# The low halves of six weight granules move from VectorE to GpSimd in the recurrence of a two-layer trunk

## The chip, the cores and the metric

The kernel runs on one core of one Trainium2 chip. The metric is the device time of one execution in microseconds (us).

## The reference

Two layers on 256 tokens of width 1024, all in float32, batch 1. Layer 0 is a gated mixer, a dense SwiGLU and a gated embedding. Layer 1 is an HGRN2 recurrence, a top-2-of-8 expert SwiGLU and a gated embedding. The change lies in the recurrence:

```python
def hgrn2(h, w_in, lb, o_norm_g, w_out):
    q, f, i, g = jnp.split(h @ w_in, 4, axis=-1)
    forget = lb + (1.0 - lb) * jax.nn.sigmoid(f)
    log_f = jnp.log(forget)
    k = 1.0 - forget
    q = jax.nn.silu(q)
...
    def step(state, inp):
        qc, kc, ic, lfc = inp
        b = jnp.cumsum(lfc, axis=2)
        o_inter = jnp.einsum('bhtk,bhkv->bhtv', qc * jnp.exp(b), state)
        attn = jnp.einsum('bhtk,bhsk,bhtsk->bhts', qc, kc, decay)
        o = o_inter + jnp.einsum('bhts,bhsv->bhtv', attn, ic)
...
    o = rms_norm(o, o_norm_g)
    return (o * jax.nn.silu(g)) @ w_out
```

## The kernel before, in words

**Weights.** Every weight matrix is streamed in granules of 128 partitions by 2048 float32 columns, in two halves of 1024 columns. For granule `g`, SyncE's queue loads each half into a slot of `raw`; ScalarE writes its rounded copy `w_hi` (`hi(g)`, L984); VectorE writes the rest, `w_lo = raw - w_hi` (`lo(g)`, L1362). TensorE multiplies three times: high by high, high by low and low by high (L460, L461, L462). The two halves of a product so keep float32's precision. `w_hi` and `w_lo` have six slots. `raw` has three before the experts begin (granule 72), so that the load of granule `g` waits for `lo_done` of granule `g - 3`. `lo_done` is one semaphore that counts halves in the order of the granules. TensorE waits for it too, and `hi(g)` waits for `used` of granule `g - 6`.

**The recurrence.** Granules 52 to 67 are its input projection (`G_INC` is 52): 52 to 55 give f, 56 to 59 q, 60 to 63 i, 64 to 67 g. Granules 68 to 71 are its output projection (`G_OUTC` is 68). The decayed products of q and k are built in levels 0 to 7, which halve the block on which they work. TensorE multiplies in a level (`level(n)`: L707 for level 0, L726 for 1 to 5, L719 for 6, L712 for 7), VectorE scales half of q and of k for the next level (L1685, L1686), signals `qk_ready`, forms the next block products (L1691), and merges the level's result into `attn` under a mask (`meet`, L1666). Between two levels TensorE has the projection of half a granule (`proj_part`, 12 matmuls). So level n + 1 waits for VectorE's two multiplications, and these wait for level n and for all that stands before them in VectorE's order. In that order stand `lo(64)` ahead of level 1's loop, and `lo(65)` to `lo(69)` at the end of the turns 2 to 6.

TensorE's order from level 3 on: level 3, half of granule 63, level 4, half of 64, level 5, half of 64, level 6, half of 65, level 7, half of 65, the products with the values (L770), the product across the two tiles (L782), and granules 66 and 67.

**GpSimd** sets constants up at the start and then issues DMAs. Its third gain is loaded once `gain_free` is 2, its fourth once `gain_free` is 3, after the recurrence's output norm.

Of the kernel before, what the change touches and what calls it, by code (L numbers as in the profile page):

```python
# [22 lines left out]
ALU = mybir.AluOpType  # L23
ACT = mybir.ActivationFunctionType
AXX = mybir.AxisListType.X
F32 = mybir.dt.float32
# [6 lines left out]
RING = 6  # L33
RAW = 3
GW = 2048
HW = GW // 2
# [7 lines left out]
def trunk(nc, x_d, pT_d, columns_d, norm_g, w_in_ab, a_ln_g, a_ln_b, wsT_d, w_out_ab, ffn_w_gu,  # L44
# [23 lines left out]
    G_INC = G_PLE0 + 5  # L68
    G_OUTC = G_INC + 16
    G_MOE = G_OUTC + 4  # L70
    assert G_MOE % RING == 0 and ITEM % RING == 0 and G_MOE % RAW == 0

    with ExitStack() as ctx:
# [7 lines left out]
        w_hi = sb("w_hi", [P, RING, GW], F32R)  # L81
        w_lo = sb("w_lo", [P, RING, GW], F32R)
# [149 lines left out]
        def raw_part(g, s):  # L232
            k = raw_slot(g)
            return raw[:, k, s * HW:(s + 1) * HW] if k < RAW else more_raw[k - RAW][:, s * HW:(s + 1) * HW]
# [19 lines left out]
        def o_bank(t):  # L254
            return 4 + 2 * t
# [125 lines left out]
        @block.gpsimd  # L381
        def _(pool):
            count = [0]

            def step(ins):

                count[0] += 1
                ins.then_inc(pool_step, 1)
                pool.wait_ge(pool_step, count[0])

            step(pool.memset(ident[:, :], 0.0))
            step(pool.affine_select(out=ident[:, :], in_=ident[:, :], compare_op=ALU.not_equal, fill=1.0, base=0,
                                    pattern=[[-1, P]], channel_multiplier=1))
            step(pool.memset(ones[:, :], 1.0))
            step(pool.affine_select(out=before[:, :], in_=ones[:, :], compare_op=ALU.is_gt, fill=0.0, base=0,
                                    pattern=[[1, P]], channel_multiplier=-1))
            pool.memset(zeros[:, :], 0.0).then_inc(consts, 1)
            pool.iota(iota_c[:, :].bitcast(I32), pattern=[[1, P]], base=0, channel_multiplier=0).then_inc(seg_in, 1)
            pool.iota(rt[:, 0:P].bitcast(I32), pattern=[[0, P]], base=0, channel_multiplier=1).then_inc(seg_in, 1)
            pool.wait_ge(lo_done, 2)  # L400
            pool.dma_start(wr[:, :, :], w_router).then_inc(router_full, 16)
            pool.dma_start(br[:, :], b_router[0:1, :].broadcast_to([P, E])).then_inc(router_full, 16)
            pool.dma_start(wsT, wsT_d).then_inc(ws_full, 16)
            pool.dma_start(lng, a_ln_g[0:1, :].broadcast_to([P, AW])).then_inc(ln_full, 16)
            pool.dma_start(lnb, a_ln_b[0:1, :].broadcast_to([P, AW])).then_inc(ln_full, 16)
            gains = [norm_g[0, 1:2], norm_g[0, 3:4], norm_g[1, 1:2], norm_g[1, 3:4]]
            for n, v in enumerate(gains):
                if n:
                    pool.wait_ge(gain_free, n)
                pool.dma_start(gain[:, :], v.broadcast_to([P, D])).then_inc(gain_full, 16)  # L410
                if n == 2:
                    pool.dma_start(ybuf[0:ROWS, :].rearrange("(p a) (b c) -> p (a b) c", p=P, c=N // 2),
                                   zeros[:, :].bitcast(F32).unsqueeze(1).broadcast_to(
                                       [P, ROWS // P * D // (N // 2), N // 2])).then_inc(rows_zero, 16)
                if n == 1:

                    pool.dma_start(pT_in, pT_d[0]).then_inc(p_full, 16)
                if n == 1:

                    pool.dma_start(vcol[:, V_ON:V_COLS], c_onorm_g[0, :].rearrange("(k p) -> p k", p=P),  # L420
                                   allow_slow_non_contiguous=True).then_inc(onorm_full, 16)
                if n == 3:

                    pool.dma_start(pT_in, pT_d[1]).then_inc(p_full, 16)


            pool.wait_ge(x_ready, x_count(3, T - 1, 1))
            pool.iota(dst, pattern=[[0, 1]], base=ROWS, channel_multiplier=1).then_inc(dst_ready, 1)
            pool.wait_ge(xn_ready, T)
            pool.dma_start(xbuf.rearrange("(t p) n -> p t n", p=P), xn[:, :, :]).then_inc(x_stored, 16)  # L430
            pool.wait_ge(rows_zero, 16)
            pool.wait_ge(x_stored, 16)
            pool.wait_ge(table_ready, 1)
            last_item = pool.value_load(itab[0:1, 0:1], min_val=E - 1, max_val=ITEMS - 1)

            def write_rows(i):
                pool.wait_ge(dst_ready, i + 1)
                pool.wait_ge(y_evac, i + 1)
                pool.sem_inc(y_seen, 1)
                pool.indirect_dma_start(ybuf[:, :], bass.IndirectOffsetOnAxis(ap=dst, axis=0), yo,  # L440
                                        None).then_inc(rows_written, 16)

            with pool.Fori(0, last_item) as i:
                pool.wait_ge(src_ready, i + 1)
                pool.wait_ge(gat_done, i * 2 + 2)
                pool.sem_inc(y_seen, 1)
                pool.indirect_dma_start(xg_rows, None, xbuf[:, :], bass.IndirectOffsetOnAxis(ap=origin, axis=0)).then_inc(x_rows, 16)
                write_rows(i)
            write_rows(last_item)
            pool.wait_ge(rows_written, last_item * 16 + 16)  # L450
            pool.wait_ge(gat_done, last_item * 2 + 2)
            pool.sem_inc(y_seen, 1)
            pool.dma_start(acc, ybuf[0:SEQ, :].rearrange("(t p) n -> p t n", p=P)).then_inc(y_loaded, 16)
            pool.dma_start(xn[:, :, :], ybuf[SEQ:ROWS, :].rearrange("(t p) n -> p t n", p=P)).then_inc(y_loaded, 16)
# [887 lines left out]
        def _(dve):  # L1342
# [14 lines left out]
            def lo(g, turns=0):  # L1357

                for s in range(2):
                    part = slice(s * HW, (s + 1) * HW)  # L1360
                    dve.wait_ge(hi_done, turns * 2 * RING + (2 * g + s + 1))
                    dve.tensor_tensor(w_lo[:, g % RING, part], raw_part(g, s), w_hi[:, g % RING, part].bitcast(F32),  # L1362
                                      ALU.subtract).then_inc(lo_done, 1)
# [309 lines left out]
            meet(0)  # L1673
            step(dve.tensor_tensor(qT, qT, fT, ALU.mult))
            dve.sem_inc(qk_ready, 1)
            lo(64)
            for lv in range(1, 8):

                width, blocks = 2 ** (lv - 1), HEADS * SEQ // 2 ** (lv - 1)
                dve.wait_ge(at_done, lv + 1)  # L1680
                pv = prev.rearrange("p (m e) -> p m e", e=2)
                q4 = qf.rearrange("p (m e w) -> p m e w", e=2, w=width)
                k4 = kf.rearrange("p (m e w) -> p m e w", e=2, w=width)
                shape = [P, blocks // 2, width]
                dve.tensor_tensor(q4[:, :, 1, :], q4[:, :, 1, :], pv[:, :, 0].unsqueeze(2).broadcast_to(shape), ALU.mult)  # L1685
                step(dve.tensor_tensor(k4[:, :, 0, :], k4[:, :, 0, :], pv[:, :, 1].unsqueeze(2).broadcast_to(shape),  # L1686
                                       ALU.mult))
                dve.sem_inc(qk_ready, 1)
                if lv < 7:
                    prev = totals[lv % 2][:, 0:blocks // 2]  # L1690
                    step(dve.tensor_tensor(prev, pv[:, :, 0], pv[:, :, 1], ALU.mult))  # L1691
                if lv < 6:
                    meet(lv)
                if lv == 5:
                    dve.sem_inc(met, 1)
                if 1 < lv < 7:
                    lo(63 + lv)

            def norm_o(t):
                dve.wait_ge(o_sq, t + 1)  # L1700
                heads = slice(t * HEADS, (t + 1) * HEADS)
                ot = oo[:, t, :].rearrange("p (h n) -> p h n", n=HD)
                step(dve.tensor_reduce(rt[:, heads], osq[t].rearrange("p (g n) -> p g n", n=HD), AXX,
                                       ALU.add))
                step(dve.tensor_scalar(nr[:, 0, heads], rt[:, heads], 1.0 / HD, EPS, ALU.mult, ALU.add))
                rsqrt(t * HEADS, (t + 1) * HEADS)
                step(dve.tensor_tensor(ot, PS[:, o_bank(t):o_bank(t) + 2, :].rearrange("p b (h n) -> p (b h) n", n=HD),
                                       nr[:, 1, heads].unsqueeze(2).broadcast_to([P, HEADS, HD]), ALU.mult))
# [7 lines left out]
            step(dve.tensor_copy(attx, PS[:, 6:8, :].rearrange("p b (h n) -> p (b h) n", h=4)))  # L1716
            dve.sem_inc(attn_ready, 1)
            norm_o(0)
            lo(70)
            gate_o(0)  # L1720
            lo(71)
# [304 lines left out]
```

## Time and profile before

| | |
|---|---|
| median of 3 runs | 1498.63 us (1494.45 to 1499.73) |
| profiled execution, first to last instruction | 1496.2 us |
| TensorE matmul busy | 1465.4 us, 98% |
| VectorE busy | 1237.6 us, 83% |
| ScalarE busy | 1004.9 us, 67% |
| GpSimd busy | 45.9 us, 3% |

The profiled execution's own time is known only as its span. It lies 2.4 us below the median of the three runs and inside their scatter. The recurrence's levels lie between 375 and 431 us of it.

### The profile page before, as it was taken

How to read it: one execution, taken by the hardware profiler on the slowest of the kernel's cores; microseconds unless marked ns; L12 is line 12 of the kernel's file. 1: busy time of each engine (PE TensorE's matmuls, PEld its weight loads, DVE VectorE, ACT ScalarE, POOL GpSimd, SP SyncE). 2: the span in 40 equal slices, each digit the busy share in tenths (PEclk: the TensorE clock that was granted, in tenths of full speed). 3: DMA queues.
4: the chain of work that ended last, by engine and by line, in shares of the span. 5: the costliest groups of instructions: out<-in, count | busy, mean ns of one | idle time of the engine just before them, and what ended most of it. 6: DMA issues, size and time to landing. Idle time of an engine off the chain costs nothing.

```text
span 1496.2 us, 23664 instructions
## 1 busy us (share of the span) xinstructions
PE 1465.4 (98%) x6903; PEld 1215.8 (81%) x6903; DVE 1237.6 (83%) x1556; ACT 1004.9 (67%) x1248; POOL 45.9 (3%) x43
## 2 busy tenths in 40 slices
PE   8999999999999999999999999999999999999998
PEld 6877888788887778888888888888888888888876
DVE  7996545674778899899989989889989889899985
ACT  6555434366236677787877877777787778778762
POOL 1000000000000120000000000000000000000000
PEclk9999999999999999999999999999999999999999
DMA  7666555456233899999999999999989999999960
GB/s 284 210 219 224 188 199 174 168 167 213 74 128 122 299 410 409 346 367 409 347 374 410 356 364 410 387 327 411 403 319 408 409 341 381 409 348 399 410 245 29
DMA packets 124631, 452.57 MB, mean 302 GB/s; under 512 B 13984, under 2 KB 13984, under 8 KB 124592
## 3 DMA queue, kind: packets, MB, share of 16 engines
q1 hardware_dynamic: 119952, 435.25, 77.4%
q0 software_dynamic: 4640, 16.82, 3.1%
q8 instruction: 22, 0.36, 0.1%
q14 instruction: 17, 0.14, 0.0%
HBM read 443.62 MB, written 8.39 MB: 302 GB/s over the span
## 4 chain that ended last, share of the span: by engine, by line
PE 89%; DVE 7%; issue 1%; ACT 1%; DMA 1%; SPq 0%; ACTq 0%; DVEq 0%
PE PS L460 28%; PE PS L462 28%; PE PS L461 28%; DVE w_lo L1362 3%; PE PS L880 2%; DMA raw<-in_w_in_ab 1%; PE PS L511 0%; PE PS L726 0%; DVE SC L1666 0%; PE PS L847 0%; ACT w_hi L984 0%; DVE SC L1685 0%; DVE SC L1686 0%; PE PS L597 0%; PE PS L834 0%
## 5 line engine op out<-in xcount | busy, mean ns | idle before, releaser
L1362 DVE TENSOR_TENSOR w_lo<-raw,w_hi 128x1024 fp32r<-128x1024 f32 x486 | 568.6, 1221 | 31.4 <-ACT w_hi L984 28.4
L460 PE MATMUL PS<-w_hi,xT_hi 128*128 128x512 f32 x1424 | 567.5, 399 | 6.1 <-DVE w_lo L1362 3.4
L462 PE MATMUL PS<-w_lo,xT_hi 128*128 128x512 f32 x1424 | 557.5, 392 | 0.0
L461 PE MATMUL PS<-w_hi,xT_lo 128*128 128x512 f32 x1424 | 556.4, 391 | 0.0
L984 ACT ACTIVATE w_hi<-raw 128x1024 fp32r<-128x1024 f32 x486 | 489.6, 1060 | 73.0 <-PE PS L462 41.8
L1362 DVE TENSOR_TENSOR w_lo<-SC,w_hi 128x1024 fp32r<-128x1024 f32 x340 | 392.0, 1220 | 8.4 <-ACT w_hi L984 6.8
L984 ACT ACTIVATE w_hi<-SC 128x1024 fp32r<-128x1024 f32 x340 | 335.7, 1061 | 12.3 <-PE PS L462 10.3
L460 PEld LDWEIGHTS PS<-w_hi,xT_hi 128*128 128x128 f32 x1424 | 269.5, 189 | 60.7 <-issue 6.3
L462 PEld LDWEIGHTS PS<-w_lo,xT_hi 128*128 128x128 f32 x1424 | 268.6, 189 | 57.8
L461 PEld LDWEIGHTS PS<-w_hi,xT_lo 128*128 128x128 f32 x1424 | 269.2, 189 | 52.9
L460 PE MATMUL PS<-w_hi,hT_hi 128*128 128x512 f32 x536 | 209.1, 390 | 3.2 <-DVE hT_lo L1580 3.2
L462 PE MATMUL PS<-w_lo,hT_hi 128*128 128x512 f32 x536 | 209.2, 390 | 0.0
L461 PE MATMUL PS<-w_hi,hT_lo 128*128 128x512 f32 x536 | 208.8, 389 | 0.0
L460 PEld LDWEIGHTS PS<-w_hi,hT_hi 128*128 128x128 f32 x536 | 100.7, 188 | 24.9 <-DVE hT_lo L1580 3.2
L462 PEld LDWEIGHTS PS<-w_lo,hT_hi 128*128 128x128 f32 x536 | 100.7, 188 | 20.9
L461 PEld LDWEIGHTS PS<-w_hi,hT_lo 128*128 128x128 f32 x536 | 100.7, 188 | 20.7
L1096 ACT ACTIVATE hT_hi<-PS 128x512 fp32r<-128x512 f32 x67 | 40.4, 603 | 95.8 <-PE PS L880 62.5
L1254 ACT ACTIVATE junk<-PS 128x512 f32<-128x512 f32 x56 | 33.5, 598 | 88.8 <-PE PS L462 88.8
L1580 DVE TENSOR_TENSOR hT_lo<-PS,hT_hi 128x512 fp32r<-128x512 f32 x67 | 46.3, 691 | 48.7 <-ACT hT_hi L1096 48.7
L1869 DVE TENSOR_TENSOR junk<-junk,PS 128x512 f32<-128x512 f32 x56 | 38.5, 687 | 28.2 <-ACT junk L1254 28.2
L880 PEld LDWEIGHTS PS<-ident,junk 128*128 128x128 f32 x224 | 35.2, 202 | 9.1 <-DVE junk L1869 5.1
L1574 DVE SCALAR_TENSOR_TENSOR junk<-PS,lbc,junk 128x256 f32<-128x256 f32 x22 | 9.6, 480 | 39.3 <-ACT junk L1090 39.3
(270 smaller groups left out, 625.8 us busy)
## 6 DMA issues: line engine op xcount, KB each, us to landing
raw<-in_e_w_gu SPq DMA_DIRECT2D x226, 512.0 KB, 8.5
SC<-in_e_w_gu SPq DMA_DIRECT2D x222, 512.0 KB, 8.3
SC<-in_e_w_down SPq DMA_DIRECT2D x114, 512.0 KB, 7.5
raw<-in_e_w_down SPq DMA_DIRECT2D x110, 512.0 KB, 7.8
raw<-in_ffn_w_gu SPq DMA_DIRECT2D x44, 512.0 KB, 4.8
raw<-in_w_in_c SPq DMA_DIRECT2D x32, 512.0 KB, 6.0
raw<-in_ffn_w_down SPq DMA_DIRECT2D x22, 512.0 KB, 5.1
raw<-in_w_in_ab SPq DMA_DIRECT2D x20, 512.0 KB, 8.5
```

What stands on the lines that cost most here:

```text
L460: pe.matmul(out, a_hi, b_hi, start=start, stop=False, skip_group_check=True)
L461: pe.matmul(out, a_lo, b_hi, start=False, stop=False, skip_group_check=True)
L462: return pe.matmul(out, a_hi, b_lo, start=False, stop=stop, skip_group_check=True)
L880: m = pe.transpose(PS[:, 2, c:c + P], hv[:, j, r, :], ident[:, :])
L984: act.activation(w_hi[:, g % RING, part], raw_part(g, s), ACT.Copy).then_inc(hi_done, 1)
L1096: act.activation(hT_hi[:, :], PS[:, b, :], ACT.Copy).then_inc(hT_act, 1)
L1254: act.activation(sg, PS[:, 0, :], ACT.Silu).then_inc(silu_done, 1)
L1362: dve.tensor_tensor(w_lo[:, g % RING, part], raw_part(g, s), w_hi[:, g % RING, part].bitcast(F32), ALU.subtract).then_inc(lo_done, 1)
L1574: m = dve.scalar_tensor_tensor(out=hh[:, cols], in0=PS[:, 2 * (b % 2) + t, 256:512], scalar=rstd(1, t), in1=sg[:, cols], op0=ALU.mult, op1 ...
L1580: dve.tensor_tensor(hT_lo[:, :], PS[:, b, :], hT_hi[:, :].bitcast(F32), ALU.subtract).then_inc(hT_ready, 1)
L1869: dve.tensor_tensor(hh, sg, PS[:, 1, :], ALU.mult).then_inc(h_ready, 1)
```

## The change

GpSimd gets a function `lo(g)` with the same two subtractions that VectorE's has. After its third gain it waits until 64 granules are done and computes `w_lo` of granules 64 to 69. VectorE's six calls are taken out, and before `lo(70)` VectorE waits until granule 69 is done. Nothing else changes.

```diff
+    POOL_LO = (G_INC + 12, G_OUTC + 2)
...
+            def lo(g):
+
+                for s in range(2):
+                    part = slice(s * HW, (s + 1) * HW)
+                    pool.wait_ge(hi_done, 2 * g + s + 1)
+                    pool.tensor_tensor(w_lo[:, g % RING, part], raw_part(g, s), w_hi[:, g % RING, part].bitcast(F32),
+                                       ALU.subtract).then_inc(lo_done, 1)
...
+                if n == 2:
+                    pool.wait_ge(lo_done, 2 * POOL_LO[0])
+                    for g in range(*POOL_LO):
+                        lo(g)
...
             dve.sem_inc(qk_ready, 1)
-            lo(64)
             for lv in range(1, 8):
...
-                if 1 < lv < 7:
-                    lo(63 + lv)
...
             norm_o(0)
+            dve.wait_ge(lo_done, 2 * POOL_LO[1])
             lo(70)
```

VectorE's order in the turns 3 to 5 of the loop over levels, before (L1685 and L1686 scale q and k in `SC` for the next level, L1691 the block products, L1666 the merge from PSUM, L1362 the low halves):

```order
L1685 TENSOR_TENSOR SC<-SC,junk 128x256x4
L1686 TENSOR_TENSOR SC<-SC,junk 128x256x4
L1691 TENSOR_TENSOR SC<-junk 128x256
L1666 COPY_PREDICATED SC<-seg,PS 128x256x4
L1362 TENSOR_TENSOR w_lo<-raw,w_hi 128x1024 x2
L1685 TENSOR_TENSOR SC<-SC 128x128x8
L1686 TENSOR_TENSOR SC<-SC 128x128x8
L1691 TENSOR_TENSOR junk<-SC 128x128
L1666 COPY_PREDICATED SC<-seg,PS 128x128x8
L1362 TENSOR_TENSOR w_lo<-raw,w_hi 128x1024 x2
L1685 TENSOR_TENSOR SC<-SC,junk 128x64x16
L1686 TENSOR_TENSOR SC<-SC,junk 128x64x16
```

The same place of the changed kernel, where L1697, L1698, L1703 and L1679 are these four and L1375 would be the low halves:

```order
L1697 TENSOR_TENSOR SC<-SC,junk 128x256x4
L1698 TENSOR_TENSOR SC<-SC,junk 128x256x4
L1703 TENSOR_TENSOR SC<-junk 128x256
L1679 COPY_PREDICATED SC<-seg,PS 128x256x4
L1697 TENSOR_TENSOR SC<-SC 128x128x8
L1698 TENSOR_TENSOR SC<-SC 128x128x8
L1703 TENSOR_TENSOR junk<-SC 128x128
L1679 COPY_PREDICATED SC<-seg,PS 128x128x8
L1697 TENSOR_TENSOR SC<-SC,junk 128x64x16
L1698 TENSOR_TENSOR SC<-SC,junk 128x64x16
L1703 TENSOR_TENSOR SC<-junk 128x64
```

Each turn loses the two rows of `w_lo` that stood between its merge and the next level's scaling; from the first row of one piece to its last the other has the same rows in the same order.

GpSimd's order around its third gain, before, with the semaphores that a row waits for:

```order
L420 DMA vcol<-in_c_onorm_g 128x8x1
L410 DMA gain<-in_norm_g 128x1024 [waits gain_free]
L412 DMA ybuf<-zeros 2048x1x256
L410 DMA gain<-in_norm_g 128x1024 [waits gain_free]
L424 DMA SC<-in_pT 128x512
```

And in the changed kernel, where L397 is the new function:

```order
L429 DMA vcol<-in_c_onorm_g 128x8x1
L419 DMA gain<-in_norm_g 128x1024 [waits gain_free]
L421 DMA ybuf<-zeros 2048x1x256
L397 TENSOR_TENSOR w_lo<-raw,w_hi 128x1024 [waits hi_done,lo_done]
L397 TENSOR_TENSOR w_lo<-raw,w_hi 128x1024 [waits hi_done] x11
L419 DMA gain<-in_norm_g 128x1024 [waits gain_free]
L433 DMA SC<-in_pT 128x512
```

The twelve subtractions stand between the zeros written to `ybuf` and the fourth gain; every one waits for ScalarE's `hi_done`, and none for VectorE once the first has started.

## Rows read from the trace of the kernel before

**Rows 1.** The page: parts 1 (busy us, share, instructions) and 4 (chain, by engine).

```profile
...
PE 1465.4 (98%) x6903; PEld 1215.8 (81%) x6903; DVE 1237.6 (83%) x1556; ACT 1004.9 (67%) x1248; POOL 45.9 (3%) x43
...
PE 89%; DVE 7%; issue 1%; ACT 1%; DMA 1%; SPq 0%; ACTq 0%; DVEq 0%
...
```

**Rows 2.** Timeline of TensorE, 374 to 438 us: start, us, line, idle before.

```profile
...
384.30 3.68 PE L726 MATMUL PS<-SC 128*128 128x64 f32 x32
387.78 0.48 PE L460 MATMUL PS<-w_hi,xT_hi 128*128 128x512 f32 x1
...
390.64 3.68 PE L726 MATMUL PS<-SC 128*128 128x64 f32 x32
...
396.98 3.71 PE L726 MATMUL PS<-SC 128*128 128x64 f32 x32
...
403.13 0.39 PE L462 MATMUL PS<-w_lo,xT_hi 128*128 128x512 f32 x1
404.91 3.79 PE L726 MATMUL PS<-SC 128*128 128x64 f32 x32 [1.39 <-DVEq L1688]
...
411.46 3.79 PE L726 MATMUL PS<-SC 128*128 128x64 f32 x32
...
424.72 2.64 PE L712 MATMUL PS<-SC 128*64 128x64 f32 x32 [2.60 <-DVEq L1688]
427.29 0.80 PE L460 MATMUL PS<-w_hi,xT_hi 128*128 128x512 f32 x1
...
428.31 0.63 PE L462 MATMUL PS<-w_lo,xT_hi 128*128 128x512 f32 x1
...
431.13 1.95 PE L770 MATMUL PS<-SC 128*128 128x128 f32 x16
...
```

**Rows 3.** Timeline of VectorE, 355 to 462 us.

```profile
...
389.16 1.22 DVE L1686 TENSOR_TENSOR SC<-SC,xn 128x1024 f32<-128x1024 f32 x1
...
395.58 1.22 DVE L1686 TENSOR_TENSOR SC<-SC 128x1024 f32<-128x1024 f32 x1
...
400.16 2.36 DVE L1362 TENSOR_TENSOR w_lo<-raw,w_hi 128x1024 fp32r<-128x1024 f32 x2
...
405.41 1.27 DVE L1666 COPY_PREDICATED SC<-seg,PS 128x1024 f32<-128x1024 uint8 x1
406.71 2.36 DVE L1362 TENSOR_TENSOR w_lo<-raw,w_hi 128x1024 fp32r<-128x1024 f32 x2
...
419.98 2.36 DVE L1362 TENSOR_TENSOR w_lo<-raw,w_hi 128x1024 fp32r<-128x1024 f32 x2 [0.52 <-DVE SC L1666]
...
423.39 1.22 DVE L1686 TENSOR_TENSOR SC<-SC 128x1024 f32<-128x1024 f32 x1
...
441.01 2.36 DVE L1362 TENSOR_TENSOR w_lo<-raw,w_hi 128x1024 fp32r<-128x1024 f32 x2
...
```

**Rows 4.** The chain that ended last, 400 to 431 us, by line.

```profile
...
by line: DVE w_lo L1362 30.5%; DVE SC L1666 20.4%; DVE SC L1686 14.8%; DVE SC L1685 14.6%; PE PS L712 8.5%; PE PS L460 5.2%; PE PS L461 3.9%; issue 3.4%; PE PS L462 2.8%; DVE SC L1691 2.2%; DVE junk L1691 1.0%; DVEq L1688 0.3%; DVEq L1695 0
...
```

**Rows 5.** A stretch of TensorE: us, busy (instructions), granted clock, DMA share, GB/s.

```profile
...
427.30:429.00 1.70, 1.70 (x5) 0.50 0.63 219
...
```

**Rows 6.** GpSimd, groups by line and shape: busy us, mean ns, idle before.

```profile
...
L397 POOL MEMSET zeros<- 128x512 bf16 x1 | 0.5, 524 | 0.1
L395 POOL TENSOR_SCALAR_AFFINE_SELECT before<-ones 128x128 f32<-128x128 f32 x1 | 0.3, 292 | 0.1
...
L2016 POOL MEMSET const-float32-0.0<- 128x1 f32 x1 | 0.1, 93 | 0.3 <-issue 0.3
```

**Rows 7.** Timeline of ScalarE, 355 to 485 us.

```profile
...
370.61 3.92 ACT L984 ACTIVATE w_hi<-raw 128x1024 fp32r<-128x1024 f32 x4
...
382.93 2.00 ACT L984 ACTIVATE w_hi<-raw 128x1024 fp32r<-128x1024 f32 x2
...
403.56 1.26 ACT L1033 ACTIVATE SC<-PS,lbc 128x512 f32<-128x512 f32 x2 [11.55 <-PE PS L462]
...
```

**Rows 8.** DMA issues, 380 to 430 us: KB each, median us to landing.

```profile
...
raw<-in_w_out_c SPq DMA_DIRECT2D x8, 512.0 KB, 4.3
...
```

## The prediction

> **What bounds the kernel now.** I read first the page's busy shares and the engines of its last chain: TensorE is busy 98% of the span and carries 89% of the chain [rows 1]. So a microsecond counts only where TensorE waits. Then TensorE's timeline through the levels, for the rows that carry a bracket. Up to level 3 it has none. Level 4 starts at 404.91 after 1.39 us of idle time, level 7 at 424.72 after 2.60 us, both released by VectorE's `qk_ready` [rows 2]. Third, the chain between 400 and 431 us alone, by line: 30.5% of these 31 us, 9.5 us, is `w_lo` on VectorE [rows 4], four granules at 2.36 us [rows 3]. The reader is to see that the two figures differ. 9.5 us lie in the chain, 3.99 us are waits. When the four go, the chain goes over to TensorE's own work, and only TensorE's idle time and what hangs on it can be won.
>
> **TensorE's own cycle.** Level 1 starts at 384.30, the next projection at 387.78, level 2 at 390.64 [rows 2]: 3.48 us for a level, 2.86 us for half a granule's projection, 6.34 us together. VectorE's two multiplications, 1.14 us from one start to the next and 1.22 us for the second, end at 390.38 for level 2 and at 396.80 for level 3 [rows 3]; TensorE starts these levels at 390.64 and 396.98. So even now the scaling ends only 0.26 and 0.18 us ahead of need. I take 0.25 us as the slack of a level.
>
> **What is removed.** Twelve subtractions leave VectorE. Granule 64's pair is hidden under level 1 and gives nothing. The pairs of granules 65 to 68 stand ahead of the scalings after levels 3 to 6 and delay them. The pair of 68 is that at 419.98, with the scaling that ends at 424.61 behind it [rows 3]; granule 69's follows that scaling, beside level 7, and gives nothing. Without the four the sequence is:
> - The scaling after level 3 starts at the level's end. TensorE's last matmul ahead of level 4 starts at 403.13 and the next could start 0.23 us later, at 403.36, where level 4 now starts at 404.91. The gain is 1.55 us.
> - Levels 5 and 6 follow at TensorE's own pace. Now level 5 starts 6.55 us after level 4 [rows 2]; 6.34 us would do. The gain is 0.2 us in each of the two cycles, together 0.4 us. VectorE then still has 2.36 us of scaling, at most 0.45 us of block products and 1.27 us of merging in a cycle of 6.34 us, so it can keep the pace.
> - The wait ahead of level 7 goes, 2.60 us.
> - The clock. After that wait the granted clock is 0.50 between 427.3 and 429 [rows 5], the 1.2 GHz level of the two, and it is back at full afterwards. Level 7 took 2.57 us from start to start, 424.72 to 427.29, and its projection 3.84 us, to 431.13 [rows 2]. Half of 2.57 is 1.28, and the projection needs 2.86 us: with no wait before it, 1.28 and 0.98 us come back.
>
> The sum is 1.55 + 0.4 + 2.60 + 1.28 + 0.98 = 6.8 us, and the products with the values, now at 431.13, would start at 424.3.
>
> **What is added on GpSimd.** Twelve subtractions of 128x1024. The trace has none on GpSimd, so I bound one. A memset of 512 elements took 524 ns and one of a single element 93 ns: 0.84 ns an element written. The affine select of 128 elements took 292 ns: 1.55 ns an element read and written [rows 6]. The floor is writing alone, 1024 x 0.84 + 93 = 0.95 us. The ceiling is twice the select's rate, 3.3 us. With a read at 1.55 - 0.84 = 0.71 ns, two reads and a write make 2.26 ns an element, 2.4 us, and I take that.
>
> GpSimd has the room. ScalarE's `w_hi` of 64 and 65 are made from 370.61 on, and TensorE needs 64 at about 407 after the change: some 35 us for four subtractions. `w_hi` of 66 starts at 382.93 [rows 7], and 67 can follow at once, since its load no longer waits for VectorE's pair at 383.8; the load takes 4.3 us [rows 8]. Those of 68 and 69 follow ScalarE's copy at 403.56 [rows 7], so GpSimd's last four run from about 406 and end near 416. VectorE asks for granule 69 ahead of `lo(70)`, now at 441.01 [rows 3] and then near 434: 18 us to spare, and the wait bites only above 7 us an operation. Loads of granules 67 to 72 wait for these halves and come earlier or at the same time. Behind the twelve stand GpSimd's fourth gain and what follows it, which wait for the output norm near 470 in any case. Their cost is nothing.
>
> **What the two engines do to each other** is the open price. GpSimd's last eight subtractions, about 384 to 394 and 406 to 416, lie beside the scalings after levels 1, 4, 5 and 6. If a scaling finds a subtraction running and has to wait for its end, it waits half of one on average: 1.2 us, less 0.25 us of slack, 0.95 us a level. Four levels make 3.8 us. From below the price is nothing; from above see the third case. The Trainium skill ("SBUF — State Buffer", section "Who interferes with whom") speaks against this change: a VectorE instruction with two SBUF inputs and a GpSimd one that reads SBUF exclude each other for the whole instruction, and the scaling has both inputs in SBUF. No row here shows the two at once. The skill's page "GPSIMD Engine Reference" (section "Elementwise — side-by-side cycle accounting") gives 4497 ns for such an operation of 2048 elements; half, an estimate of 2.25 us, would move the four levels' price to 3.5 us.
>
> **The cases.**
> - A, the engines don't disturb each other: 6.8 us won, 1491.8. For it: each engine's rate in the trace has no sign of a shared resource, but none could show. Chance 0.30.
> - B, a scaling waits for the subtraction that is running and nothing more: 6.8 - 3.8 = 3.0 us won, 1495.6. Chance 0.38, the likeliest, because its price lies between nothing and C's and needs nothing to go a special way; the skill's rule would give it or C.
> - C, they take turns: between a scaling's two multiplications another subtraction is let in. It is slower. In eight subtractions some four then fall whole ahead of a multiplication on the chain: 4 x 2.4 - 3 x 0.3 of slack = 8.7 us against 6.8, so 1.9 us slower, 1500.5; at 3.3 us an operation 12.3 against 6.8, 1504.1. It decides from 1.9 us an operation upward. For it: the scaling's slack is so small that nothing absorbs a turn. Against it: the two multiplications run back to back, 1.14 us apart, with no gap in which another could enter. Chance 0.22.
> - D, the chain is shortened here and the time comes back as a wait further on. TensorE shows no bracket from 425 to the output projection [rows 2] and everything behind hangs on its progress, so little speaks for it: 1498.6. Chance 0.10.
>
> **How the numbers follow.** The base is the median 1498.6; the profiled execution's span, 1496.2, from which the durations come, is 2.4 us below it and within the runs' scatter. The forecast is B, 1495.6, with 1492 to 1499 as its own range. The range for everything goes from A less that 2.4 us, 1489.5, to C with an operation of nearly 3 us, 1502.5. Half a per cent is 7.5 us, about what a measurement of this kernel can tell from no change. A's 6.8 us lie just inside: of its 0.30 I put a third beyond, and 0.04 of B's, so 0.14 for faster; slower takes 0.06, C's upper end and a surprise in an operation of 4 us; the rest is the same.
>
> **What the changed profile would show.** Under A, TensorE has no bracket from level 1 to level 7, level 4 starts near 403.4 and the products with the values near 424.3 at full clock. Under B, VectorE's multiplications (1.22 us each now) show single ones of 2 to 3.5 us, and the values start near 428. Under C, both of a pair are long, and level 2 already starts later than 390.64, near 393. GpSimd's row should show twelve of 1 to 3.3 us; above 4 us the forecast is wrong in all cases that have a disturbance. It is wrong too if TensorE waits for `lo_done` or VectorE at `lo(70)`, or if the clock falls in another place.

## The result, and the profile after

The changed kernel takes 1504.53 us (median of 5 runs, 1503.47 to 1505.83), the kernel before 1497.89 us (5 runs). The ratio is 1.0043, with a 95% interval of 1.0029 to 1.0056: 6.6 us slower. The forecast was 1495.6 us, in a range of 1489.5 to 1502.5. The profiled execution spans 1504.1 us, against 1496.2.

GpSimd's twelve subtractions, grouped (busy us, mean ns of one, idle before):

```profile
L397 POOL TENSOR_TENSOR w_lo<-raw,w_hi 128x1024 fp32r<-128x1024 f32 x12 | 32.1, 2706 | 99.0 <-ACT w_hi L997 99.0
```

and in order of time (start, us for the whole group):

```profile
372.13 9.41 POOL L397 TENSOR_TENSOR w_lo<-raw,w_hi 128x1024 fp32r<-128x1024 f32 x4 [78.24 <-ACT w_hi L997]
384.36 11.32 POOL L397 TENSOR_TENSOR w_lo<-raw,w_hi 128x1024 fp32r<-128x1024 f32 x4 [2.81 <-ACT w_hi L997]
413.61 11.34 POOL L397 TENSOR_TENSOR w_lo<-raw,w_hi 128x1024 fp32r<-128x1024 f32 x4 [17.93 <-ACT w_hi L997]
```

The first four, beside which VectorE has no instruction with two inputs in SBUF, take 2.35 us each. The other two fours take 2.83 us each on average, and single ones up to 3.37 us (shortest, median and longest, in ns):

```profile
L397 POOL TENSOR_TENSOR w_lo<-raw,w_hi x12: 2352/2408/3373, 372.1 to 422.5; 128x1024 fp32r<-128x1024 f32 x12
```

The timeline of VectorE after levels 1 and 4 shows the other side (L1697 and L1698 scale q and k, L1703 forms the block products, L1679 merges):

```profile
388.30 1.86 DVE L1697 TENSOR_TENSOR SC<-SC,xn 128x1024 f32<-128x1024 f32 x1 [4.36 <-PE PS L739]
390.09 3.38 DVE L1698 TENSOR_TENSOR SC<-SC,xn 128x1024 f32<-128x1024 f32 x1
393.61 3.15 DVE L1703 TENSOR_TENSOR SC<-xn 128x1024 f32<-128x1024 f32 x1
...
414.97 2.11 DVE L1697 TENSOR_TENSOR SC<-SC 128x1024 f32<-128x1024 f32 x1 [2.13 <-PE PS L739]
417.00 3.37 DVE L1698 TENSOR_TENSOR SC<-SC 128x1024 f32<-128x1024 f32 x1
420.53 2.20 DVE L1703 TENSOR_TENSOR junk<-SC 128x128 f32<-128x128 f32 x1 [0.15 <-DVE SC L1698]
422.77 1.26 DVE L1679 COPY_PREDICATED SC<-seg,PS 128x1024 f32<-128x1024 uint8 x1
```

They are turns, instruction by instruction. GpSimd's second subtraction of the group at 384.36 ends near 389.0 (two of 2.35 us). VectorE's L1697, issued at 388.30, ends 1.1 us after that. The third then ends near 392.4, and L1698, issued at 390.09, ends 1.1 us after that, at 393.47. L1703 has the fourth ahead of it. A multiplication that found the other engine idle took 1.22 us [rows 3]; here one takes 3.38. L1679 at 422.77, with one input in PSUM, runs beside GpSimd's last subtraction in its usual 1.26 us.

TensorE's timeline shows what it costs (L739 is levels 1 to 5, L732 level 6, L725 level 7, L783 the products with the values):

```profile
384.59 3.68 PE L739 MATMUL PS<-SC 128*128 128x64 f32 x32
...
393.58 7.09 PE L739 MATMUL PS<-SC 128*128 128x64 f32 x32 [2.49 <-DVEq L1700]
...
404.81 3.68 PE L739 MATMUL PS<-SC 128*128 128x64 f32 x32
...
411.12 3.73 PE L739 MATMUL PS<-SC 128*128 128x64 f32 x32
...
420.49 6.84 PE L739 MATMUL PS<-SC 128*128 128x64 f32 x32 [2.81 <-DVEq L1700]
...
431.86 1.21 PE L732 MATMUL PS<-SC 128*32 128x32 f32 x64
...
435.96 2.08 PE L725 MATMUL PS<-SC 128*64 128x64 f32 x32
...
440.83 1.95 PE L783 MATMUL PS<-SC 128*128 128x128 f32 x16
```

The waits ahead of levels 4 and 7 [rows 2] are gone, as forecast. In their place there are two new ones, 2.49 us ahead of level 2 and 2.81 us ahead of level 5, and these two levels take 7.09 and 6.84 us where the others take 3.7. The granted clock of TensorE in stretches (us, busy, clock, DMA share, GB/s) says why:

```profile
391.00:393.60 2.60, 0.11 (x2) 0.98 0.49 158
393.60:397.00 3.40, 3.40 (x16) 0.50 0.45 154
397.00:400.70 3.70, 3.70 (x19) 0.50 0.41 137
400.70:402.00 1.30, 1.30 (x4) 0.50 0.00 0
...
420.50:424.00 3.50, 3.50 (x18) 0.54 0.51 166
...
427.30:431.90 4.60, 4.60 (x15) 0.59 0.13 46
```

After each wait it runs at 1.2 GHz for nearly the whole level and most of the projection, about 10 us each time. From level 1 to the products with the values the kernel before needs 46.8 us (384.30 to 431.13, [rows 2]), the changed one 56.2 us: 9.4 us more in this stretch.

The two spans differ by 7.9 us: level 1 starts 0.3 us later, the stretch is 9.4 us longer, and what follows it is 1.8 us shorter. That last part is the clock again. Near 487 us, behind the recurrence, the kernel before falls to 1.2 GHz for a while (first row, granted clock 0.72 over 6 us), and at the same place of the changed kernel, some 10 us later, the clock stays at full (second row):

```profile
486.00:492.00 6.00, 5.72 (x31) 0.72 1.00 339
```

```profile
495.00:502.00 7.00, 6.16 (x50) 1.00 1.02 336
```

### The profile page after: what moved, and what is told of

The parts are those of the page before. It is cut to its first block, busy times and chain, and to the rows that moved or that the text cites. A ratio compares the mean times of both kernels' runs of the same rounds, so it can differ in the third digit from the quotient of the medians.

```text
span 1504.1 us, 23663 instructions
## 1 busy us (share of the span) xinstructions
PE 1472.6 (98%) x6901; PEld 1221.6 (81%) x6903; DVE 1233.6 (82%) x1544; ACT 1004.4 (67%) x1248; POOL 78.1 (5%) x55
## 4 chain that ended last, share of the span: by engine, by line
PE 87%; DVE 9%; DMA 1%; issue 1%; ACT 1%; SPq 0%; ACTq 0%; DVEq 0%
PE PS L473 27%; PE PS L475 27%; PE PS L474 27%; DVE w_lo L1375 3%; PE PS L893 2%; PE PS L739 2%; DMA raw<-in_w_in_ab 1%; ACT w_hi L997 1%; PE PS L524 0%; DVE SC L1698 0%; PE PS L860 0%; DMA raw<-in_e_w_gu 0%; DVE nr L1401 0%; PE PS L610 0%; DVE SC L1697 0%
## 5 line engine op out<-in xcount | busy, mean ns | idle before, releaser
L1375 DVE TENSOR_TENSOR w_lo<-raw,w_hi 128x1024 fp32r<-128x1024 f32 x474 | 554.4, 1219 | 31.4 <-ACT w_hi L997 29.3
L997 ACT ACTIVATE w_hi<-raw 128x1024 fp32r<-128x1024 f32 x486 | 489.2, 1060 | 62.2 <-PE PS L475 41.9
L1375 DVE TENSOR_TENSOR w_lo<-SC,w_hi 128x1024 fp32r<-128x1024 f32 x340 | 391.9, 1219 | 8.5 <-ACT w_hi L997 6.8
L460 POOL DMA_INDIRECT SC<-xbuf,seg x7 | 15.8, 2253 | 717.2 <-DVE seg L1907 717.2
```

The lines of the kernel that those rows point to most:

```text
L997: act.activation(w_hi[:, g % RING, part], raw_part(g, s), ACT.Copy).then_inc(hi_done, 1)
```

## The experiments

Each ratio is to the kernel before, with its 95% interval. "The stretch" is the time from the start of level 1 to the start of the products with the values, in the one profiled execution of each.

**1. Subtractions of 2 columns.** Of each of GpSimd's twelve subtractions 2 of 1024 columns are left, so most of six granules' low halves is left out.

```diff
-                    pool.tensor_tensor(w_lo[:, g % RING, part], raw_part(g, s), w_hi[:, g % RING, part].bitcast(F32),
+                    few = slice(s * HW, s * HW + 2)
+                    pool.tensor_tensor(w_lo[:, g % RING, few], raw_part(g, s)[:, 0:2], w_hi[:, g % RING, few].bitcast(F32),
```

> The changed kernel, with GpSimd's twelve subtractions cut to 2 of their 1024 columns, so most of the low halves of granules 64 to 69 is left out. Theory (the two engines exclude each other for a whole instruction, and TensorE's waits that this makes then cost clock): no subtraction is long enough to block, VectorE's multiplications are 1.22 us each, TensorE has no wait between level 1 and level 7, the products with the values come 40.5 us after level 1 instead of 56.2, and the time is 6 us below the kernel before, ratio 0.996. Rival (the extra wait on lo_done or the longer program costs, not the overlap): the time stays at 1.004 of the kernel before.

Measured: 1491.11 us against 1498.58, ratio 0.9955 (0.9941 to 0.9969), stretch 40.8 us. TensorE's timeline has no bracket in it:

```profile
384.73 3.68 PE L740 MATMUL PS<-SC 128*128 128x64 f32 x32
...
391.07 3.68 PE L740 MATMUL PS<-SC 128*128 128x64 f32 x32
...
410.16 3.71 PE L740 MATMUL PS<-SC 128*128 128x64 f32 x32
...
416.61 1.21 PE L733 MATMUL PS<-SC 128*32 128x32 f32 x64
...
420.69 2.08 PE L726 MATMUL PS<-SC 128*64 128x64 f32 x32
```

The kernel has every wait and every signal of the changed one. So these cost nothing, and the loss lies in the subtractions themselves. The stretch is 6.0 us shorter than before's: this is what the removal from VectorE can give. GpSimd's short subtractions show the exclusion from its side. Ten of the twelve take 0.20 us; the two issued while VectorE scales take 0.75 and 0.93 us and end within 0.1 us of the multiplication that was running:

```profile
408.14 0.75 POOL L398 TENSOR_TENSOR w_lo<-raw,w_hi 128x2 fp32r<-128x2 f32 x1 [0.75 <-ACT w_hi L998]
409.10 0.93 POOL L398 TENSOR_TENSOR w_lo<-raw,w_hi 128x2 fp32r<-128x2 f32 x1 [0.21 <-ACT w_hi L998]
```

```profile
407.61 1.23 DVE L1698 TENSOR_TENSOR SC<-SC 128x1024 f32<-128x1024 f32 x1 [2.14 <-PE PS L740]
408.75 1.22 DVE L1699 TENSOR_TENSOR SC<-SC 128x1024 f32<-128x1024 f32 x1
```

**2. GpSimd writes only.** Three memsets stand in for each subtraction; `w_lo` of the six granules is zero.

```diff
-                    pool.tensor_tensor(w_lo[:, g % RING, part], raw_part(g, s), w_hi[:, g % RING, part].bitcast(F32),
-                                       ALU.subtract).then_inc(lo_done, 1)
+                    for r in range(2):
+                        step(pool.memset(w_lo[:, g % RING, part].bitcast(F32), 0.0))
+                    pool.memset(w_lo[:, g % RING, part].bitcast(F32), 0.0).then_inc(lo_done, 1)
```

> The changed kernel, with each of GpSimd's twelve subtractions replaced by three memsets of the same 1024 columns, about 3 us together, so the low halves of granules 64 to 69 are zeros. GpSimd is as busy beside VectorE as before and writes as much, but reads nothing. Theory (it is GpSimd's reads that exclude VectorE's instructions with two inputs in SBUF): multiplications stay at 1.22 us, ratio to the kernel before 0.996. Rival (any use of SBUF by GpSimd excludes them): multiplications of 2 us and more, ratio 1.000 to 1.005.

Measured: 1490.16 us, ratio 0.9944 (0.9928 to 0.9960), stretch 40.8 us. GpSimd and then VectorE, in order of time:

```profile
387.17 1.97 POOL L398 MEMSET w_lo<- 128x1024 f32 x2
389.19 0.96 POOL L399 MEMSET w_lo<- 128x1024 f32 x1
390.09 1.97 POOL L398 MEMSET w_lo<- 128x1024 f32 x2
```

```profile
388.22 1.23 DVE L1698 TENSOR_TENSOR SC<-SC,xn 128x1024 f32<-128x1024 f32 x1 [4.36 <-PE PS L740]
389.36 1.22 DVE L1699 TENSOR_TENSOR SC<-SC,xn 128x1024 f32<-128x1024 f32 x1
```

GpSimd is busy without a gap, and the multiplications have their 1.22 us. A busy GpSimd that only writes doesn't touch VectorE; it is the subtraction's reads.

**3. One input instead of two.** GpSimd multiplies the raw half by 0.5.

```diff
-                    pool.tensor_tensor(w_lo[:, g % RING, part], raw_part(g, s), w_hi[:, g % RING, part].bitcast(F32),
-                                       ALU.subtract).then_inc(lo_done, 1)
+                    pool.tensor_scalar(w_lo[:, g % RING, part], raw_part(g, s), 0.5, None, ALU.mult).then_inc(lo_done, 1)
```

> The changed kernel, with GpSimd multiplying the raw half by 0.5 in place of the subtraction, so w_lo of granules 64 to 69 is wrong; it reads one input from SBUF where the subtraction reads two and the memsets none. Theory (any read of GpSimd excludes VectorE's two-input instruction): multiplications that meet it are longer by its duration, some 1 to 1.6 us, and the ratio lies between those of the memsets (0.994) and the subtractions (1.004), near 0.997 if TensorE's waits stay short. Rival (only two-input instructions of both engines exclude each other): multiplications of 1.22 us, ratio 0.995.

Measured: 1491.76 us against 1499.02, ratio 0.9959 (0.9942 to 0.9975), stretch 41.9 us. GpSimd's operation is longer than the subtraction, 2.77 us where nothing holds it up and 2.97 us on average, yet every scaling has 1.22 us:

```profile
384.79 11.67 POOL L397 TENSOR_SCALAR w_lo<-raw 128x1024 fp32r<-128x1024 f32 x4 [1.17 <-ACT w_hi L996]
```

```profile
388.73 1.23 DVE L1696 TENSOR_TENSOR SC<-SC,xn 128x1024 f32<-128x1024 f32 x1 [4.36 <-PE PS L738]
389.88 1.22 DVE L1697 TENSOR_TENSOR SC<-SC,xn 128x1024 f32<-128x1024 f32 x1
391.24 1.83 DVE L1702 TENSOR_TENSOR SC<-xn 128x1024 f32<-128x1024 f32 x1
```

My expectation of the theory failed here, and the rival's is nearly met: a read of one input doesn't exclude VectorE's multiplication for its length. The two engines still hold each other up. Three of GpSimd's twelve operations, those issued while the second scaling of a pair runs, take 3.45 to 3.67 us:

```profile
L397 POOL TENSOR_SCALAR w_lo<-raw x12: 2763/2776/3669, 372.6 to 416.0; 128x1024 fp32r<-128x1024 f32 x12
```

And the block products, behind a gap of 0.15 us, are 0.6 us longer in the same three turns (1.83 for 1.22 here). Why VectorE is held up there and not in the scalings, this run doesn't tell.

**4. Quarters.** Each subtraction in four of 256 columns, the signal on the last.

```diff
+                    for q in range(4):
+                        piece = slice(s * HW + q * 256, s * HW + (q + 1) * 256)
+                        m = pool.tensor_tensor(w_lo[:, g % RING, piece], raw_part(g, s)[:, q * 256:(q + 1) * 256],
+                                               w_hi[:, g % RING, piece].bitcast(F32), ALU.subtract)
+                    m.then_inc(lo_done, 1)
```

> The changed kernel, with each of GpSimd's subtractions cut into four of 256 columns, some 0.6 us each, so that VectorE's multiplication waits for a quarter at a time. Theory (turns by whole instructions): each multiplication that meets GpSimd is delayed by one short one, some 0.6 us instead of 2.1, so the waits ahead of levels 2 and 5 fall to under 1 us, the clock stays at full, and the time is 3 to 6 us below the kernel before, ratio 0.996 to 0.998. Rival (GpSimd keeps the port from one instruction to the next, or the two share it in proportion): multiplications of 2 to 3.4 us as in the changed kernel, ratio near 1.004.

Measured: 1495.81 us, ratio 0.9981 (0.9970 to 0.9992), stretch 45.1 us. The multiplications behind level 5:

```profile
416.37 1.82 DVE L1700 TENSOR_TENSOR SC<-SC,junk 128x1024 f32<-128x1024 f32 x1 [1.98 <-PE PS L742]
418.12 1.76 DVE L1701 TENSOR_TENSOR SC<-SC,junk 128x1024 f32<-128x1024 f32 x1
```

The delay is about 0.55 us each instead of 2.15: it goes with the length of GpSimd's instruction. Ahead of every level from 1 to 7 but the fourth TensorE waits 0.23 to 1.25 us, and no level behind them is longer than 3.79 us. The stretch flatters this run, because its first wait, of 0.78 us, lies ahead of level 1, behind a VectorE instruction that takes 3.76 us where the kernel before has 2.29. From level 0 on the profiled execution gains 0.8 us over the kernel before, and not 1.7; the rest of its 2.7 us is the time at 1.2 GHz near 487 us, which it doesn't have. Same work, same engines, and the loss is gone, but the gain inside the recurrence is small.

**5. Dummy matmuls in the two waits.** The changed kernel, with matmuls that fill TensorE's waits.

```diff
             proj_part(10, 1)
+            pe.wait_ge(i_evac, 1)
+            warm(12, 0)
             level(2)
...
             proj_part(12, 0)
+            pe.wait_ge(i_evac, 2)
+            warm(13)
             level(5)
```

> The changed kernel, with dummy matmuls into a free PSUM bank ahead of levels 2 and 5, 12 and 13 of them of 512 columns, that fill TensorE's two waits of 2.5 and 2.8 us. VectorE and GpSimd do as before. Theory (of the changed kernel's loss the larger part is the clock that falls after the two waits, 4.9 us of level 2 with the projection behind it and 4.9 us of level 5 with its own): the granted clock stays at full, levels 2 and 5 take 3.5 us, and the time is 8 to 10 us below the changed kernel, ratio to the kernel before 0.998 to 1.0. Rival (the levels are long because of something that GpSimd or VectorE does to them): they stay near 7 us and the ratio near 1.004.

Measured: 1499.69 us, ratio 1.0017 (1.0005 to 1.0030), stretch 48.9 us.

```profile
393.31 3.79 PE L739 MATMUL PS<-SC 128*128 128x64 f32 x32
...
401.50 3.79 PE L739 MATMUL PS<-SC 128*128 128x64 f32 x32 [1.58 <-DVEq L1704]
...
417.32 3.79 PE L739 MATMUL PS<-SC 128*128 128x64 f32 x32
```

Level 2 comes 9.00 us after level 1, as in the changed kernel (8.99), but takes 3.79 instead of 7.09 us, and so does level 5. The long levels were the clock. 7.3 us of the stretch come back (56.2 less 48.9), 4.8 us by the two medians, 3.9 us by the two ratios, against 8 to 10 expected; the ratio lies above the 0.998 to 1.0 expected too. Part was hidden before: VectorE itself is late after level 1, with the block products and the merge pushed back, and level 3 now waits 1.58 us for it.

**6. Two granules.** Only 64 and 65 on GpSimd, 66 to 69 on VectorE as before.

```diff
-    POOL_LO = (G_INC + 12, G_OUTC + 2)
+    POOL_LO = (G_INC + 12, G_INC + 14)
...
+                if 2 < lv < 7:
+                    if lv == 3:
+                        dve.wait_ge(lo_done, 2 * POOL_LO[1])
+                    lo(63 + lv)
```

> The changed kernel, with only granules 64 and 65 on GpSimd, whose subtractions run before the first scaling, and 66 to 69 back on VectorE at the ends of turns 3 to 6. Theory: VectorE's multiplications are 1.22 us each, the wait ahead of level 4 (1.39 us) is gone and that ahead of level 7 (2.6 us, with its clock) stays, so 1.4 to 1.6 us are gained, ratio 0.999. Rival (GpSimd's use costs in itself): ratio 1.001 and above.

Measured: 1493.20 us, ratio 0.9966 (0.9953 to 0.9980), stretch 43.3 us. Its four subtractions take 2.38 us and end before the first scaling. The wait ahead of level 4 is gone, and the one ahead of level 7 is 2.25 us:

```profile
423.27 2.08 PE L725 MATMUL PS<-SC 128*64 128x64 f32 x32 [2.25 <-DVEq L1700]
```

The stretch is 3.5 us shorter than before's, more than expected, since after this wait the clock did not fall: 2.08 us for level 7 where the kernel before has 2.64 [rows 2].

**7. All six on VectorE, where it is idle.** Nothing on GpSimd.

```diff
             dve.sem_inc(qk_ready, 1)
+            los(64, 66)
...
             dve.sem_inc(qk_ready, 1)
-            lo(64)
+            lo(66)
             for lv in range(1, 8):
...
-                if 1 < lv < 7:
-                    lo(63 + lv)
+                if lv > 5:
+                    lo(61 + lv)
...
+            lo(69)
             dve.wait_ge(at_done, 9)
```

> The kernel before, with all six granules on VectorE, but at places where it is idle: 64 and 65 ahead of the merge of level 0, 66 where 64 stood, 67 beside level 7, 68 and 69 behind the last scaling. GpSimd does nothing. Theory (what the forecast promised, TensorE's waits gone, needs no second engine): no wait between level 1 and level 7, full clock, 6 us below the kernel before, ratio 0.996, and the same as with GpSimd's work cut to 2 columns. Rival (the later pairs of 67 to 69 hold up a load or the output norm): waits of TensorE after level 7, ratio 0.998 to 1.002.

Measured: 1492.09 us, ratio 0.9957 (0.9943 to 0.9971), stretch 40.8 us, and no bracket in it. VectorE had been idle for 15.8 us ahead of the first merge, and two granules fit there:

```profile
372.19 4.63 DVE L1362 TENSOR_TENSOR w_lo<-raw,w_hi 128x1024 fp32r<-128x1024 f32 x4 [8.45 <-ACT w_hi L984]
```

Granules 64 to 66 have moved to earlier places here and 67 to 69 to later ones. It beats both kernels: the whole gain of experiment 1, with all the work done.

**8. The kernel before with 12 dummy matmuls ahead of level 7.**

```diff
             proj_part(13, 0)
+            pe.wait_ge(i_evac, 2)
+            warm(12)
             level(7)
```

> The kernel before, with 12 dummy matmuls of 512 columns into a free PSUM bank ahead of level 7, where TensorE waits 2.60 us. VectorE's work is untouched. Theory (the clock falls because of that wait, and the changed kernel's GpSimd-free traces show level 7 at 2.01 us from start to start at full clock): level 7 takes 2.0 instead of 2.57 us and the projection behind it 2.9 instead of 3.84, 1.5 us gained, ratio 0.999. Rival (the prediction's own figure): level 7 takes 1.3 us, 2.3 us gained.

Measured: 1496.44 us against 1499.02, ratio 0.9989 (0.9977 to 1.0001): no clear difference. Level 7 is 2.08 us long, and 2.08 is its length in every run at full clock, so the 1.3 us of the prediction was wrong. It halved the level's time as if all of it had been at 1.2 GHz; the kernel before's granted clock over it was 0.75:

```profile
424.70:427.30 2.60, 2.58 (x33) 0.75 0.56 191
```

The profiled execution of this experiment also showed the following:

```profile
406.00 5.47 PE L726 MATMUL PS<-SC 128*128 128x64 f32 x32 [1.40 <-DVEq L1690]
```

The wait of 1.4 us ahead of level 4 has cost clock here, and not in the kernel before [rows 2]. The stretch is 48.2 us.

**9. The kernels once more.** Three single executions, each profiled: two of the kernel before and one of the changed kernel.

> The kernel before once more, unchanged, one profile. Theory (TensorE's wait of 1.4 us ahead of level 4 costs clock in some executions and not in others): the stretch from level 1 to the products with the values takes either 46.8 us, as in the first profile, or some 3 us more with level 4 at a granted clock of one half. Rival (the extra length of level 4 seen with the dummy matmuls ahead of level 7 came from these): always 46.8 us.

> The kernel before a third time, for the same question: 46.8 us or some 3 us more.

> The changed kernel once more, unchanged, one profile. Theory: VectorE's instructions have the same lengths to within 0.1 us (1.9 and 3.4 us after level 1, 2.1 and 3.4 us after level 4), and the stretch from level 1 to the products with the values is 56.2 us, or less by up to 5 us where one of the two waits doesn't cost clock. Rival (the lengths are chance): other multiplications are long.

Measured: 1495.35, 1499.19 and 1503.97 us; the stretches are 46.8, 46.8 and 54.5 us. The kernel before has the same stretch in three of three, as the rival says: that the wait of 1.4 us ahead of level 4 cost clock is seen only in experiment 8. But the dummy matmuls start some 20 us after level 4 does, so that they caused it is not shown, and a single profile may be chance. That one program can go either way is seen behind the recurrence. After a wait of 1.49 us near 486 us the clock fell in two profiles of the kernel before and stayed at full in the third, the first of this experiment:

```profile
486.00:492.00 6.00, 5.09 (x40) 1.00 1.02 319
```

In the changed kernel VectorE's instructions agree within 0.1 us:

```profile
388.22 1.83 DVE L1697 TENSOR_TENSOR SC<-SC,xn 128x1024 f32<-128x1024 f32 x1 [4.36 <-PE PS L739]
389.97 3.38 DVE L1698 TENSOR_TENSOR SC<-SC,xn 128x1024 f32<-128x1024 f32 x1
```

TensorE's level 2 took 5.99 us this time instead of 7.09. The turns are fixed by the program; how much clock they cost is not.

## Why the prediction was wrong

**What is removed** held in kind: TensorE's waits, not VectorE's 9.5 us, are what can be won, and experiments 1 and 7 show it. The size was 6.0 us in the stretch for 6.8 forecast. The term that was off is level 7, taken as half of 2.57 us; it needs 2.0 us from start to start at full clock, so 0.6 us come back and not 1.28.

**What is added** held, but for the times: 2.35 us a subtraction alone for 2.4 us, GpSimd's room, the loads and the wait at `lo(70)`. The last four subtractions ran from 413.6 to 425.0 and not from 406 to 416, since the levels ahead of them had become longer. A memset of 1024 columns took 0.954 us, where the floor was 0.95.

**What the two engines do to each other** is the step that failed. The likeliest case had a scaling wait for the running subtraction and nothing more, 0.95 us a level in four levels. The traces show case C. The argument against it, that the two multiplications leave no gap in which another instruction could enter, is false: GpSimd's pending subtraction goes in between two multiplications that run back to back. A turn needs no gap. The rule in the Trainium skill ("SBUF — State Buffer", section "Who interferes with whom") on two-input VectorE instructions beside a GpSimd instruction that reads agrees with experiments 1 and 2 and with the 3.38 us; that the scalings keep 1.22 us in experiment 3, where GpSimd reads one input, does not follow from it.

**Case C** was priced at 1.9 us slower and is 6.6. It had the delay of the scalings at 8.7 us. TensorE's waits for them are 5.6 us, counted from the end of the projections (2.65 ahead of level 2, which comes 8.99 us after level 1 instead of 6.34, and 2.96 ahead of level 5). This part was overrated: the subtractions meet only the scalings after levels 1 and 4, and the levels after 5 see none. What was missing is the clock. The prediction gave back the clock that the wait ahead of level 7 had cost and charged none for the new waits, in any of the cases. This term was put at nothing without a reason, and it is the second step that failed: C's own sum, with no clock in it, gives 1500.5 us, inside the stated range. Levels 2 and 5 with the projections behind them take 11.23 and 11.37 us, against 6.34 and 6.45 us in experiment 1: 9.8 us. 5.6 + 9.8 = 15.4 us, the whole difference between the stretches of the changed kernel (56.2) and of experiment 1 (40.8). Against the kernel before, which has 6.0 us of its own waits and clock there, it is 9.4 us.

The stretch says 9.4 us, or 7.7 in the second profile, the two spans 7.9 us and the medians 6.6 us. The first and the spans differ by the time at 1.2 GHz near 487 us, which two of three profiles of the kernel before show, and neither of the two of the changed kernel. The 1.3 us between spans and medians lie within the scatter of single runs (1494.45 to 1499.73 for the kernel before).

**The rivals.** A gives the right figure for a GpSimd that doesn't read two inputs, but not for this change. D is excluded: experiments 1 and 7 keep the 6.0 us to the end of the run (6.5 to 7.5 us by the medians).

## What to carry to other kernels

Work moved from VectorE to GpSimd isn't parallel when both instructions take two inputs from SBUF: they take turns by whole instructions, also between two that run back to back. Put such work where VectorE is idle or reads PSUM, or cut GpSimd's instructions short, which here turned a loss of 0.4% into a gain of 0.2%, though part of the gain may be clock behind the recurrence. Before a second engine is used, look for idle time of the first ahead of the critical loop: here 15.8 us lay open, and earlier places for three granules and later ones for three gave all that the removal could give. And price a new wait of TensorE with the clock behind it: here the clock cost 9.8 us after 5.6 us of waits.

## What the runs showed of the hardware

- A subtraction of two 128x1024 float32 inputs takes GpSimd 2.35 us where nothing holds it up, a product with a constant 2.77 us (experiment 3), a memset 0.95 us (experiment 2). The one with a single input is the slowest of them.
- The exclusion works both ways: a subtraction of 2 columns, 0.20 us elsewhere, took 0.75 and 0.93 us beside VectorE's scalings (experiment 1).
- VectorE's predicated copy and its products with one input in PSUM run beside GpSimd's subtraction at their usual length (1.26 us for the copy at 422.77; 2.29 us for the product with the identity at 379.33, as before).
- TensorE's clock after a wait of similar length differs. After 2.25 us (experiment 6) it stayed at full; after 2.60 us (before) it fell for some 4 us; after 2.49 and 2.81 us (changed kernel) for about 10, and in a second profile, after 2.47 us, for about 7; after 1.40 us it stayed in the kernel before and fell in experiment 8; after 1.49 us near 486 us it fell in two profiles of the kernel before and stayed in one.
